# A two-layer hybrid diffusion block: the recurrence's preparation is put ahead of each projection unit, and the chunked recurrence gets a product of values and states in one, and a first inverse by transposes

## What is computed

```python
p = p + mu * (0.5 * (pp[:, :-2] + pp[:, 2:]) - p)               # mix with both neighbours
w_log = -softplus(-(w0 + einsum('btdr,drc->dbtc', tanh(zw), w2))) - 0.5
decay = exp(-exp(w_log))
a = sigmoid(a0 + einsum('btdr,drc->dbtc', za, a2))
kk = kkf / maximum(sqrt(sum(kkf * kkf)), 1e-12)
...
S = S * w_t - (S @ kk_t) b_t + v_t k_t ;  y_t = S @ r_t          # per head (64x64), two directions
```

## Time and profile before

| | |
|---|---|
| median of 3 runs | 2534.96 us (2534.52 to 2537.42) |
| profiled execution | 2525.96 us, its span 2524.2 us |
| PE busy over the span | 2158.9 us, 86% |
| PEld, DVE, ACT, POOL | 72%, 51%, 36%, 29% |
| common stage of layer 0 | 0 to 658 us; the next stage's first DMA at 671.6 us |
| recurrence | 671.6 to about 1205 us |

### The profile page before, as it was taken

The page is one execution under the profiler, slowest core; times in us unless marked ns, Lnnn a source line. Parts: engine busy times, 40 slices in busy tenths (PEclk is TensorE's granted clock), DMA queues, the critical chain, the costliest instruction groups (busy, mean ns, idle before and its releaser), DMA issues. The chain is left out here.

```text
span 2524.2 us, 57280 instructions
## 1 busy us (share of the span) xinstructions
PE 2158.9 (86%) x24254; PEld 1823.0 (72%) x24254; DVE 1291.5 (51%) x2064; ACT 905.5 (36%) x1765; POOL 723.2 (29%) x786
## 2 busy tenths in 40 slices
PE   3899997798179999998699994993899969999988
PEld 1666885576169989998588884773787758888866
DVE  4335467976435555554354444975546424444322
ACT  2223144455245555553133332223333303333311
POOL 2246322211143342431050001443457415000012
PEclk6999998899589999999699996996999979999989
DMA  8555444553422122110421106534344453111062
GB/s 300 184 145 155 132 146 147 187 175 120 149 77 79 54 79 78 55 58 16 96 92 34 43 13 195 182 115 162 109 114 103 112 140 117 51 51 51 32 205 92
DMA packets 207036, 280.46 MB, mean 111 GB/s; under 512 B 39640, under 2 KB 145016, under 8 KB 205760
## 3 DMA queue, kind: packets, MB, share of 16 engines
q1 hardware_dynamic: 168736, 171.52, 22.4%
q0 software_dynamic: 25680, 81.58, 10.2%
q10 hardware_dynamic: 12368, 23.70, 3.1%
HBM read 188.78 MB, written 87.95 MB: 110 GB/s over the span
## 5 line engine op out<-in xcount | busy, mean ns | idle before, releaser
L164 PE MATMUL in_acc<-in_hi,in_whi 128*128 128x512 f32 (+1 forms) x1024 | 401.3, 392 | 19.9 <-DVE in_lo L840 17.9
L164 PE MATMUL in_acc<-in_lo,in_whi 128*128 128x512 f32 (+1 forms) x1024 | 380.3, 371 | 0.0
L164 PE MATMUL in_acc<-in_hi,in_wlo 128*128 128x512 f32 (+1 forms) x1024 | 380.1, 371 | 0.0
L164 PEld LDWEIGHTS in_acc<-in_hi,in_whi 128*128 128x128 f32 x1024 | 199.5, 195 | 72.7 <-issue 42.5
L164 PEld LDWEIGHTS in_acc<-in_lo,in_whi 128*128 128x128 f32 x1024 | 199.7, 195 | 35.4 <-issue 5.3
L164 PEld LDWEIGHTS in_acc<-in_hi,in_wlo 128*128 128x128 f32 x1024 | 198.9, 194 | 33.3
L1935 DVE TENSOR_REDUCE dense_top<-dense_score 128x1 f32<-128x640 f32 (+1 forms) x144 | 112.3, 780 | 163.1 <-PE dense_score L2022 163.1
L1935 DVE TENSOR_REDUCE window_top<-window_score 128x1 f32<-128x640 f32 (+1 forms) x128 | 101.2, 791 | 179.5 <-PE window_score L2018 179.5
L2060 PEld LDWEIGHTS dense_outs<-dense_V,dense_p 128*128 128x128 f32 x1344 | 170.3, 192 | 8.5 <-ACT dense_p L1903 4.9
L2060 PE MATMUL dense_outs<-dense_V,dense_p 128*128 128x65 f32 x1344 | 170.7, 270 | 0.9 <-ACT dense_p L1903 0.8
L2060 PE MATMUL window_outs<-window_V,window_p 128*128 128x65 f32 x1216 | 157.6, 273 | 1.6 <-ACT window_p L1903 1.1
(11 more groups left out here) (269 smaller groups left out, 5085.6 us busy)
## 6 DMA issues: line engine op xcount, KB each, us to landing
streams<-in_streams_out POOLq DMA_DIRECT2D x40, 512.0 KB, 3.8
scan_L<-streams SPq DMA_DIRECT2D x80, 256.0 KB, 3.7
in_wl<-in_w_mod ACTq DMA_DIRECT2D x32, 512.0 KB, 4.4
in_raw<-in_w_in_even SPq DMA_DIRECT2D x28, 512.0 KB, 4.3
in_raw<-in_w_in_odd SPq DMA_DIRECT2D x20, 512.0 KB, 3.8
close_ga<-gates SPq DMA_DIRECT2D x18, 512.0 KB, 4.3
in_wm<-in_w_mod SPq DMA_DIRECT2D x8, 1024.0 KB, 12.2
gates<-in_outs POOLq DMA_DIRECT2D x32, 256.0 KB, 3.5
```

The source lines that it names most:

```text
L164: last = pe.matmul(out, a(k), b(k), start=(k == 0 and x == 0), stop=(k == n - 1 and x == 2))
```

## The change

In the common stage: `jobs0` puts five mix jobs first, then keys, values and queries, then the other nine mix jobs, then all eight gate jobs (before: two gates, keys, values, queries, 14 mixes, six gates). Slots begin at unit 38, are spread evenly up to unit 84, and every engine does a unit's slots **ahead of** the unit's other work. An item passes through more slots: PE makes its loras three slots early, ACT its rates one slot early, DVE its running sum in slot t, ACT the exponentials in t+1, DVE the products in t+2. Both loras of an item now contract the same row half d and write one bank; the banks freed serve norms and values in turn (`three`). The rates before the step (`before`) are no longer subtracted on DVE but read from the exponentials shifted by one (`falls`, 65 places for 64), and (a-1)k_a+1 is made by ACT instead of DVE. `clear` also fills `falls`.

In the recurrence: `first` turns XT by four transposes with the identity instead of 16 products of 64x64, and ACT copies the result in four parts. Values and state share a tile V (values in one row half, state in the other), and U holds under each unit, in the same halves, the part for the values and the part for the state, so that z makes of L1685 and L1687 one product over 128 rows. DVE writes the state's part of U (`eq`) in two halves. `load_values` issues four DMAs instead of two.

```diff
-    CLEAR_AT, N_AT = 36, 40
+    CLEAR_AT, N_AT, FLUSH = 36, 38, 3
...
-        slot_of_unit[u] = min(len(items) + 1, max(0, min(u - N_AT, NSG) + max(0, (u - N_AT - NSG) * 27 // 20)))
+        slot_of_unit[u] = min(len(items) + FLUSH, max(0, u - N_AT) * (len(items) + FLUSH) // (NU + 1 - N_AT))
...
 ACT slot(t)
-                    if item(t)[0] == "X":
-                        rates(*item(t)[1:])
-                    if item(t)[0] == "N":
-                        root_keys(*item(t)[1:])
+                    if item(t + 1)[0] == "X":
+                        rates(*item(t + 1)[1:])
+                    if item(t - 2)[0] == "N":
+                        root_keys(*item(t - 2)[1:])
...
 PE
-                    half, other = slice(d * HD, (d + 1) * HD), slice((1 - d) * HD, (2 - d) * HD)
...
-                    pe.matmul(aux[:, h, 0:SG], w2s[half, pair], tz[half, cols], start=True, stop=True).then_inc(lora_w, 1)
-                    pe.matmul(aux[:, 2 + h, 0:SG], a2s[other, pair], za[other, cols], start=True, stop=True).then_inc(lora_a, 1)
+                    pe.matmul(aux[:, n % 2, 0:SG], w2s[half, b * P:(b + 1) * P], tz[half, s * SG:(s + 1) * SG], start=True, stop=True
+                              ).then_inc(lora_w, 1)
...
+                    pe.matmul(aux[:, n % 2, SG:2 * SG], a2s[half, b * P:(b + 1) * P], za[half, s * SG:(s + 1) * SG], start=True, stop=True
+                              ).then_inc(lora_a, 1)
...
                 for what, i in order:
                     if what == "T":
                         turn(i)
                     else:
+                        for t in slots(what, i):
+                            slot(t)
                         if i < NU:
                             product(i)
...
-                    for t in slots(what, i):
-                        slot(t)
...
 chunked_scan, PE
-                    for u, c in pairs():
-                        last = pe.matmul(small[s][half_of(c), u, :], XT[j % 3][half_of(1 - c), u, :], eye[half_of(1 - c), :],
-                                         start=True, stop=True)
+                    for v in range(0, NU, 2):
+                        last = pe.transpose(small[s][:, v:v + 2, :].rearrange("p a n -> p (a n)"),
+                                            XT[j % 3][:, v:v + 2, :].rearrange("p a n -> p (a n)"), ident[:])
...
-                            for n in range(3):
-                                for d in range(2):
-                                    u, half = unit(h, d, g), half_of(x ^ d)
-                                    to = sums[d][:, x, h * 2 + g, :]
-                                    if n == 0:
-                                        pe.matmul(to, U[j % 4][half, u, 0, :], PD[s][half, u, HD:P], start=True, stop=False)
-                                    elif n == 1:
-                                        pe.matmul(to, U[j % 4][half, u, 1, :], values_of(j, u, half), start=False, stop=False)
-                                    else:
-                                        last = pe.matmul(to, EQ[s][half, u, :], state[half, d, r, h * 2 + g, :], start=False, stop=True)
+                            for d in range(2):
+                                u, c = unit(h, d, g), x ^ d
+                                pe.matmul(sums[d][:, x, h * 2 + g, :], U[j % 4][half_of(c), u, place(c, 0), :], PD[s][half_of(c), u, HD:P],
+                                          start=True, stop=False)
+                            for d in range(2):
+                                u, c = unit(h, d, g), x ^ d
+                                last = pe.matmul(sums[d][:, x, h * 2 + g, :], U[j % 4][:, u, place(c, 1), :],
+                                                 values_of(j, u, c, slice(0, P)), start=False, stop=True)
...
-    jobs0 = (gates[:2] + key_jobs(QC, AKV, kst0) + value_jobs(QC + AKV * HD, AKV, v0) + query_jobs(0, AH, qst0, 3) + mixes
-             + gates[2:])
+    jobs0 = (mixes[:5] + key_jobs(QC, AKV, kst0) + value_jobs(QC + AKV * HD, AKV, v0) + query_jobs(0, AH, qst0, 3) + mixes[5:]
+             + gate_jobs(GA, gates0, 3))
```

More of the change, by code:

```diff
@@ L232, in slots @@
             return range(0)
-        return range(slot_of_unit[i], len(items) + 1 if i == NU + 3 else slot_of_unit[i + 1])
+        return range(slot_of_unit[i], slot_of_unit[i + 1])
     def item(t):
@@ L242, in q_of @@
         return b * NSG + s
+    side_uses = [("N", 0, 0)] if decay else []
+    for t in range(len(items)):
+        if item(t + 1)[0] == "N":
+            side_uses.append(item(t + 1))
+        if item(t - 1)[0] == "X" and item(t - 1)[3] == 1:
+            side_uses.append(("V", *item(t - 1)[1:3]))
+    if decay:
+        side_uses.append(("V", PAIRS - 1, NSG - 1))
     with Stage(nc, name) as st:
@@ L358, in which_of, with side_of, free_side @@
             return 0 if t < NTX else 1
+        def side_of(use, c=None):
+            to = three[side_uses.index(use) % 3]
+            return to[:, 0:SG] if c is None else to[:, c * P:(c + 1) * P]
+        def free_side(eng, use):
+            m = side_uses.index(use)
+            if m < 3:
+                return
+            what, b, s = side_uses[m - 3]
+            eng.wait_ge(clamped if what == "N" else values_read, q_of(b, s) + 1)
         def free_xs(eng, u):
@@ L475, in _ @@
                     for b in range(PAIRS):
-                        done = unit_of(items.index(("N", b - 1, NSG - 1)) + 1) + 1 if b else 0
+                        done = unit_of(items.index(("N", b - 1, NSG - 1)) + 2) + 1 if b else 0
                         loads.append((max(CLEAR_AT + 1, ready(2 + 3 * b), done), 2, load_keys, (b,)))
@@ L785, in _ @@
                         continue
+                    for t in slots(what, i):
+                        if item(t - 2)[0] == "X":
+                            store_streams(*item(t - 2)[1:])
                     if is_kind(i - 1, "rope"):
@@ L799, in _ @@
                         store_heads(i - 3)
-                    for t in slots(what, i):
-                        if item(t - 1)[0] == "X":
-                            store_streams(*item(t - 1)[1:])
                 n_mix = sum(job["kind"] == "mix" for job in jobs)
```

242 lines of the change are left out of this document (127 added, 115 removed).

## The result

| | before | after |
|---|---|---|
| median | 2534.5 us (2531.4 to 2537.4, 5 runs) | 2588.5 us (2586.8 to 2608.0, 5 runs) |
| ratio | | 1.0233 (95%: 1.0195 to 1.0270) |
| last product of the common stage, last DVE work | 626, 657.3 us | 639.8, 641.3 us |
| first product of the recurrence | 679.0 us | 662.8 us |
| last product of the recurrence | 1200.6 us | 1262.7 us |

The kernel is 54 us slower, where +10 was forecast. The profiled execution of after is 2608 us, 20 us above its median; dense attention takes 318 us in it as before (319), but the windowed attention near the end takes 366 us for 348, at a lower clock. So I read the two changed stages from it and nothing behind them: the first gives 16 us, the second takes 78.

The account below looks back on a forecast made before the run. PE was taken to bound the recurrence; in the common stage, waits and a tail of slots were to be won. Common stage -25 and recurrence +35 gave +10 us on 2535, so 2545 us, range 2508 to 2570.

Parts of the forecast that it names:

- Common stage, -25 us: Whole common stage: fewer PE waits and a shorter tail, -25 us, between -45 and -5.
- Where the slots begin: Common stage, ahead of unit 38: later stores of unit 32 make PE stand 17 us, plus 2 us at half clock.
- PE's work from there: Common stage from the slots' start: 46 units, X items, norms' sums and values' transposes take PE 279 us.
- ACT's table loads: Common stage: 36 table loads instead of 17, 24 us more on ACT; PE's waits 19 us, between 5 and 35.
- The end: End of the common stage: last slots done 5 us behind PE's 630, at 635 instead of 658 us.
- z, +38 us: z in the recurrence: no pass saved, seven more changes of form a z at 0.137 us, +38 us for 40 z.
- Rivals 2 and 3: Changes of form cost nothing inside z, 2506 us, chance 0.11; z paid by number of products, about 2470 us, 0.02.
- Other edits: nothing: Recurrence: DVE writing the state's part of U in two halves costs nothing; bare, it would be 1.4 us a group.
- first, -9 us: `first` in the recurrence: four transposes take 0.45 us for 0.87 or 0.93, -0.46 us each, -9 us for 20.
- ACT's copy, +3: Recurrence, behind `first`: ACT's four copies take 0.9 us more, about 0.3 us bare; +3 us, between 0 and 8.
- Start, +4 us: Start of the recurrence: seven more DMAs ahead of the third group's streams, 0.7 us each at most, +4 us.

Follow-up runs that it names:

- experiment 1: The kernel before with the change's common stage and its new order of jobs alone; 0.9897 times the kernel before.
- experiments 3 and 4: The changed kernel with z's products grouped by form, over all heads, then within two heads only; 0.9989 and 1.0041 times the kernel before.
- Experiment 6: The kernel before with the sums of `eq` put out on the opposite half and DVE adding the identity in two crossing halves; 1.0055 times before, +14 us.
- 8: The changed kernel with z grouped by form and p and U's first places moved, so `eq` reads and writes one half; 0.9942 times the kernel before.
- first_turned: The kernel before with `first` alone turned by four transposes and four copies on ACT; 0.9986 times the kernel before.
- scan_only: The kernel before with the change's recurrence alone; 1.0265 times the kernel before, +67 us.
- mended: The kernel of experiment 8: z grouped by form and `eq` back in the quarters that y and av leave free; 0.9942 times the kernel before.
- eq_swapped: The kernel of Experiment 6: the kernel before with the sums of `eq` put out on the opposite half; 1.0055 times the kernel before.
- z_grouped: The changed kernel with z's half-array products of all heads first, its products over 128 rows behind them; 0.9989 times the kernel before.

## Why the prediction was off

The direction was right, the size was not: +54 us for +10, outside the range. By its own steps:

- **Common stage, -25 us: right in sum** (-26 by experiment 1, -16 to -20 by the starts of the recurrence in two traces). Its parts were off both ways, so that the sum came out is in part luck. *Where the slots begin*: PE was to stand 17 us ahead of unit 38, it stood 9.1 (313.5 to 322.7 us). The step "its stores land at 288.5 + 20.4 + 3.2 = 312 us" failed: SP began at 306.90 as before, and its 12 loads took 9.1 us, not 11. *PE's work from there*: 317 us from 322.7 to 639.8, where 279 + 19 were forecast. The listed waits behind the start are 17.0 + 5.4 + 4.3 = 27 us; the remaining 290 are 11 over the term, and seven units behind waits, each 1.0 to 2.1 us longer at the half clock, account for them. *ACT's table loads*: 36 were forecast and 37 stand in the trace from the first slot on, before 17; the waits were to be 19 us in all and are 27, of which 17.0 for ACT's rates. *The end*: the last slots are 1.5 us behind the last product, not 5.
- **z, +38 us: right.** +1.01 us a z at the full clock, 40 times, +40 us; a change of form costs 0.144 us (experiments 3 and 4) for the 0.137 assumed, and passes are indeed not saved: 24 of 0.112 us before and after. Rivals 2 and 3 fell by the same rows. (By the prediction's own terms the recurrence of rival 2 would be -3 us, not -4.)
- **"Other edits: nothing": the step that failed.** The prediction counted DVE's two halves of the state's part of U, and didn't ask what the merged product had moved to make room for it: the output half of `eq`. Before, `eq` ran in the quarters (rows c, columns c) beside y and av in (rows c, columns 1 - c); now it queues with them, 0.64 to 1.83 us a period, +24 us of PE's row in 20 periods. Experiment 6 shows this mechanism alone and 8 undoes it; in time they are worth +14 and -12 us, since waits of PE shrink or come back beside it, so how much of the 24 counts depends on what else fills the period. The view was at hand: the before-rows above stand in the trace that I read, and that two half-array products share a pass was an argument of the prediction itself.
- **The clock, not in the prediction at all.** Two z at 7.84 instead of 7.66 us and x with xt at 5.37 instead of 5.03 are 0.5 us a period, some +9 us over the regular ones; counted by the eight periods of 28.0 for 26.5 us it's 12. It went when six, or four, of the eight changes of form in a z were taken out (experiments 3 and 4, one trace each); why the changes bring it isn't shown. The earlier trace rows showed full clock, and I took it as given for the changed kernel too.
- **first, -9 us, and ACT's copy, +3**: the stretch fell by 0.37 us a period, -7 us, but alone it gave nothing measurable. ACT's copies cost PE 1.2 us of waits in ten periods of `first_turned`, 2.4 in 20, near the +3 forecast. **Start, +4 us**: the wait for the third group's streams ends 52.8 us after the recurrence's first product (715.62 - 662.80) instead of 48.1 (727.04 - 678.99), so +4.7, as forecast; that the seven added DMAs are the cause wasn't tried.

The terms of the recurrence, from the traces: z 40, `eq` 24, clock 9, `first` -7, start 6 (from the first product to the first z 79.9 us for 74.1), and -5 for waits of before that shrank: +67 us, which is also the difference of the medians in `scan_only`. That is a count as if all 20 periods were full ones. The profiled recurrences differ by more, 598 against 522 us: 6 to the first z, 57 from there to the fifth z before the last, and 14 in the drain behind it, which takes 55 us for 41, where groups run out and less stands beside z and `eq`. That the count and the medians agree so well is therefore partly chance.

The Trainium skill, page "TensorEngine Tiling (Array Packing)", section "Key Properties", says that tiles operate independently, each tied to its partitions, and that a change of mode drains TensorE. Both halves are what this case turns on: the earlier trace rows and experiments 3 and 4 agree with the second, experiment 6 with the first.

What stays open: the gaps of 0.5 to 2.3 us without a releaser that come up once PE's period nears 24 us (6.4 us in 240 of before, 6.0 in one group of `mended`, at most 1.3 in `eq_swapped`). They cap what a shorter row of PE can give, and no experiment asked for their cause. Open, too, are why the clock falls without a gap ahead of it, and the 13 to 18 us between the whole change and the sum of its two stages.

## What to carry to other kernels

Where an edit moves an operand or a result to another half of the array, list which quarters each product beside it in the queue uses: two that shared a pass may now take turns, though neither costs more by itself. Merging products of two forms pays only if it saves passes; if forms must mix, group all of one form first, since each change has its price (0.144 us here), and with eight in a z the clock fell here as well. And when PE asks for another engine's result earlier, that engine's own order has to move with it: here that was worth more than anything else in the change.

## What the runs showed that was not expected

- The granted clock fell to half in the middle of work that counts as busy throughout (0.80, 0.50, 0.85 in three stretches of 2 us from 908 us on). In the two traces with eight changes of form a z this comes eight times each up to 1190 us; where other traces show a fall in the regular periods, PE had stood for 1.5 to 2.3 us just before.
- Four records of 64x128 and eight of 64x64 that want the same quarters take 0.24 + 0.23 us; in separate quarters the twelve take about 0.22 us together (the rows of before: two and four from 906.66 to 906.77).
- A sum of several products can be opened once for a whole bank: in `z_grouped` the first head's product opens it and the other heads' first products follow without. That is what let the forms be grouped.
